# A two-layer hybrid encoder on one core: split matmuls reordered over PSUM banks, with a fourth pair of split weight buffers

## The chip, the cores and the metric

The kernel runs on one core of a Trainium2 chip. The metric is the device time of one execution in microseconds; lower is better. TensorE multiplies (the trace keeps its weight loads apart as PEld), VectorE (DVE), ScalarE (ACT) and GpSimd (POOL) do the rest, and SyncE (SP) issues the DMAs. PSUM has eight banks, named 0 to 7 in the code (`pb[b]`).

## What is computed

Two layers (`DEPTH = 2`), 512 tokens, width 1024, all in float32:

```python
n = rms_norm(h, norm_mix[l]);  p = n @ w_in[l]
h = h + concat(mla(p), gla(p), hgrn2(p)) @ w_mix_out[l]
h = h + memory_cross_attention(rms_norm(h), rms_norm(mem), ...)   # 4 heads, 256 memory tokens
gate, up = split(rms_norm(h) @ w_ffn_in[l])                       # 2 x 2816 columns
h = h + (silu(causal_conv3(gate) + b) * up) @ w_ffn_out[l]
```

The mixer has three parts: a latent attention with low-rank q and kv, and two gated linear recurrences.

## The kernel before, in words

**Products in three parts.** A float32 product is made from two numbers for each operand, hi (`fp32r`, what TensorE keeps of the value) and lo (the rest). `product` (line 594) issues three matmuls into one bank, one after the other: hi x hi (line 597), hi x lo (line 598), lo x hi (line 599). The trace names them by these lines. Each matmul has its own weight load.

**Weight slabs.** The weights come as a list of slabs (`slabs`, lines 89 to 175) of at most 1024 columns per partition, in the order of use. A slab goes through three steps, each on its own engine:

- SP loads it into one of RAW = 3 raw buffers (line 511) as soon as the slab three back has been split;
- ScalarE copies it to `w_hi` (line 938), when the slab SPLIT = 3 back is released, that is, when TensorE has issued its last matmul with it;
- GpSimd subtracts to get `w_lo` (line 552), and only then may TensorE use the slab (`use`, line 588).

ScalarE and GpSimd do this between their other work, in an order written out by hand. `ahead(name)` (line 941) in ScalarE's program splits up to slab `name + SPLIT - 1`, which waits for the release of the slab before `name`.

**Who multiplies.** Two helpers do nearly all of the split products:

- `feature_chunk` (line 619) makes 128 output features for all 512 tokens in one bank: 8 steps of k, 24 matmuls in a row into the same bank. It makes the latents, the features of the recurrences, and the FFN's gate and up chunks. In the FFN there are two groups g of 11 pairs; pair n writes the banks 4g + 2(n mod 2) for gate and the next one for up (lines 912 to 919), each finished and released by itself.
- `token_group` (line 630) makes up to 512 output columns for each of four token tiles t (two for the memory) in four banks. For each k it goes through the tiles, with three matmuls for each, so the bank changes every third matmul. It makes the q, kv, v, r (`br`) and c,i,g (`cig`) projections, the mix, cross-attention and FFN outputs.

`claim(b)` waits until bank b has been read by its last reader. In a token group it stands before a tile's first product. A tile's last product signals its reader: VectorE adds the bank to h (`add_to_h`, line 1284), or ScalarE copies it out.

**The q/k stage.** Behind the kv projections VectorE prepares q and k for eight token tiles in turn (lines 1317 to 1367), and ScalarE makes a small step for each (line 1058); before each of these steps stands one `ahead` (lines 1050 to 1058). Meanwhile TensorE makes the features, then the v, r and c,i,g groups. The r group uses banks 0 to 3, of which bank 1 is read by VectorE (line 1360) in this chain. After the c,i,g group ScalarE evicts it (lines 1088 to 1091) and TensorE turns q and k.

**The FFN round.** For a chunk n VectorE multiplies the gate bank by the norm (line 1493), makes the convolution (lines 1495 to 1498), reads the up bank (line 1501), multiplies (line 1503) and makes a_lo (line 1505). ScalarE's program for n is: `ahead(gate)`, `ahead(up)`, silu (line 1208), a_hi (line 1210).

Elsewhere: `transpose_h` (line 601) turns h after the additions for the next norm; `y_ready` (line 837) turns the recurrences' output before the second half of k in the mix projection.

Of the kernel before, what the change touches and what calls it, by code (L numbers as in the profile page):

```python
# [27 lines left out]
def build_trunk(nc, A, out):  # L28
# [11 lines left out]
    P = 128  # L40
# [3 lines left out]
    NT, KD, MT = SEQ // P, D // P, NM // P  # L44
# [12 lines left out]
    FCG = FC // FG  # L57
# [31 lines left out]
    slabs, slab_at = [], {}  # L89
# [83 lines left out]
        for half in range(2):  # L173
            half_of(("ffo", g), A["w_ffn_out"], FCG, half, k0=g * FCG)
    NS = len(slabs)
    RAW, SPLIT, SLAB = 3, 3, 1024

    with ExitStack() as ctx:

# [37 lines left out]
        x_hi = place("x_hi", 0, [P, KD, SEQ], f32r)  # L217
        x_lo = place("x_lo", 16, [P, KD, SEQ], f32r)
# [65 lines left out]
        pb = [ctx.enter_context(nc.psum_tensor(f"bank{i}", [P, 512], f32)) for i in range(8)]  # L284
# [12 lines left out]
        S = {n: ctx.enter_context(nc.semaphore(n)) for n in names}  # L297
# [190 lines left out]
        with nc.Block() as block:  # L488
# [82 lines left out]
            released = {}  # L571

            @block.tensor
            def _(pe):
                freed, count = {}, {}

                def mark(ins, sem):

                    ins.then_inc(sem, 1)
                    count[id(sem)] = count.get(id(sem), 0) + 1  # L580
                    return sem, count[id(sem)]

                def claim(b):

                    if b in freed:
                        pe.wait_ge(*freed[b])

                def use(name):
                    i = slab_at[name]
                    nk, cols, _ = slabs[i]  # L590
                    pe.wait_ge(S["lo_split"], i + 1)
                    return [w[i % SPLIT][:, 0:nk * cols].rearrange("p (k c) -> p k c", k=nk) for w in (w_hi, w_lo)]

                def product(o, a, b, first, last):

                    (ah, al), (bh, bl) = a, b
                    pe.matmul(o, ah, bh, start=first, stop=False)  # L597
                    pe.matmul(o, ah, bl, start=False, stop=False)  # L598
                    return pe.matmul(o, al, bh, start=False, stop=last)  # L599
# [19 lines left out]
                def feature_chunk(name, b, w, done, evac, cols=P):  # L619

                    claim(b)
                    wh, wl = use(name)
                    for k in range(KD):
                        pe.wait_ge(S["x_lo_done"], w * KD + k + 1)
                        mm = product(pb[b][0:cols, :], (wh[:, k, :], wl[:, k, :]), (x_hi[:, k, :], x_lo[:, k, :]),
                                     k == 0, k == KD - 1)
                    released[slab_at[name]] = mark(mm, done)
                    freed[b] = evac

                def token_group(names, b0, cols, x, k0, ready, done, evac, nt=NT, before={}):  # L630

                    xh, xl = x
                    nk_all = sum(slabs[slab_at[n]][0] for n in names)
                    k = 0
                    for i, n in enumerate(names):
                        if i in before:
                            before[i]()
                        wh, wl = use(n)
                        for kk in range(slabs[slab_at[n]][0]):
                            if ready is not None:  # L640
                                pe.wait_ge(*ready(k))
                            for t in range(nt):
                                if k == 0:
                                    claim(b0 + t)
                                mm = product(pb[b0 + t][:, 0:cols],
                                             (xh[:, k0 + k, t * P:(t + 1) * P], xl[:, k0 + k, t * P:(t + 1) * P]),
                                             (wh[:, kk, :], wl[:, kk, :]), k == 0, k == nk_all - 1)
                                if k == nk_all - 1:
                                    last = mark(mm, done)
                            k += 1  # L650
                        released[slab_at[n]] = last if k == nk_all else mark(mm, S["slab_used"])
                    for t in range(nt):
                        freed[b0 + t] = (evac[0], evac[1] + t + 1)
# [59 lines left out]
                for t in range(NT):  # L713
                    mm = pe.transpose(pb[6][:, t * ROPE:(t + 1) * ROPE], rope_lr[0:ROPE, t * P:(t + 1) * P], ident[0:ROPE, 0:ROPE])
# [197 lines left out]
                for g in range(FG):  # L912
                    for c in range(FCG):
                        n = g * FCG + c
                        b = 4 * g + 2 * (n % 2)
                        feature_chunk(("gate", g, c), b, 2, S["ffn_mm"], (S["gate_ready"], n + 1))
                        feature_chunk(("up", g, c), b + 1, 2, S["ffn_mm"], (S["act_ready"], n + 1))
                        if n == 0:
                            spread_r(1)
                    for half in range(2):  # L920
                        project(("ffo", g), FCG, lambda k: (S["a_lo_done"], g * FCG + k + 1), (a_hi, a_lo),
                                (2 + g) * H_ADDS, half)
# [620 lines left out]
```

## Time and profile before

| | |
|---|---|
| median of 3 runs | 1568.45 us (1568.07 to 1570.29) |
| profiled execution: span from first to last instruction | 1568.1 us |
| profiled execution: time around the span | not listed apart; its span equals the lowest run to 0.1 us |
| TensorE busy | 1477.2 us, 94% |
| VectorE, ScalarE, GpSimd busy | 783.0, 596.9 and 638.7 us |
| granted TensorE clock | 0.982 of 2.4 GHz on average |

The busy time of TensorE counts matmuls that overlap each other, each from its start to the modelled end of its last column; two starts of neighbours are nearer to each other than one matmul is long. The pace is therefore read from starts, and the standstills from the gaps. A row's bracket names the idle time before it and what ended it.

### The profile page before, as it was taken

How to read it: one execution, taken by the hardware profiler on the slowest of the kernel's cores; microseconds unless marked ns; L12 is line 12 of the kernel's file. 1: busy time of each engine (PE TensorE's matmuls, PEld its weight loads, DVE VectorE, ACT ScalarE, POOL GpSimd, SP SyncE). 2: the span in 40 equal slices, each digit the busy share in tenths (PEclk: the TensorE clock that was granted, in tenths of full speed). 3: DMA queues.
4: the chain of work that ended last, by engine and by line, in shares of the span. 5: the costliest groups of instructions: out<-in, count | busy, mean ns of one | idle time of the engine just before them, and what ended most of it. 6: DMA issues, size and time to landing. Idle time of an engine off the chain costs nothing. (4 is left out here: it accounts for less than half of the span.)

```text
span 1568.1 us, 18614 instructions
## 1 busy us (share of the span) xinstructions
PE 1477.2 (94%) x6967; PEld 1196.0 (76%) x6967; DVE 783.0 (50%) x1505; ACT 596.9 (38%) x1053; POOL 638.7 (41%) x338
## 2 busy tenths in 40 slices
PE   6997889999999999999989898889999999999997
PEld 5886657787788888888868775678867888888886
DVE  4289468335376504653133965772345663055620
ACT  5524554457433212232154146633564322122220
POOL 5433621453343444444335254423523444444342
PEclk9998999999999999999999899999999999999999
DMA  5322001332233233333143220012322332333321
GB/s 146 96 80 68 27 1 41 94 108 68 81 94 94 88 101 95 94 94 100 35 118 95 68 81 1 1 65 84 118 68 70 95 106 88 90 106 89 99 87 74
DMA packets 172975, 125.81 MB, mean 80 GB/s; under 512 B 11825, under 2 KB 149840, under 8 KB 172880
## 3 DMA queue, kind: packets, MB, share of 16 engines
q1 hardware_dynamic: 172880, 124.56, 26.7%
q8 instruction: 58, 0.95, 0.2%
q14 instruction: 37, 0.30, 0.1%
HBM read 122.44 MB, written 2.10 MB: 79 GB/s over the span
## 5 line engine op out<-in xcount | busy, mean ns | idle before, releaser
L552 POOL TENSOR_TENSOR w_lo<-raw,w_hi 128x1024 fp32r<-128x1024 f32 (+2 forms) x230 | 544.5, 2371 | 789.2 <-ACT w_hi L938 789.1
L938 ACT ACTIVATE w_hi<-raw 128x1024 fp32r<-128x1024 f32 (+2 forms) x230 | 236.7, 1033 | 354.6 <-PE bank L599 349.0
L597 PE MATMUL bank<-x_hi,w_hi 128*128 128x512 f32 (+1 forms) x880 | 349.7, 397 | 0.3 <-DVE x_lo L1221 0.3
L598 PE MATMUL bank<-x_lo,w_hi 128*128 128x512 f32 (+1 forms) x880 | 347.8, 395 | 0.0
L599 PE MATMUL bank<-x_hi,w_lo 128*128 128x512 f32 (+1 forms) x880 | 347.8, 395 | 0.0
L597 PEld LDWEIGHTS bank<-x_hi,w_hi 128*128 128x128 f32 (+1 forms) x880 | 164.7, 187 | 41.7 <-issue 1.0
L598 PEld LDWEIGHTS bank<-x_lo,w_hi 128*128 128x128 f32 (+1 forms) x880 | 164.7, 187 | 41.0 <-issue 1.0
L599 PEld LDWEIGHTS bank<-x_hi,w_lo 128*128 128x128 f32 (+1 forms) x880 | 164.7, 187 | 40.7
L597 PE MATMUL bank<-w_hi,x_hi 128*128 128x512 f32 (+1 forms) x448 | 168.7, 376 | 18.7 <-POOL w_lo L552 12.5
L1289 DVE TENSOR_TENSOR h<-h,bank 128x512 f32<-128x512 f32 x64 | 44.0, 688 | 250.3 <-PE bank L599 250.2
L599 PE MATMUL bank<-w_hi,x_lo 128*128 128x512 f32 (+1 forms) x448 | 165.2, 369 | 0.0
L598 PE MATMUL bank<-w_lo,x_hi 128*128 128x512 f32 (+1 forms) x448 | 165.2, 369 | 0.0
L599 PE MATMUL bank<-w_hi,a_lo 128*128 128x512 f32 x352 | 138.7, 394 | 0.0
L598 PE MATMUL bank<-w_lo,a_hi 128*128 128x512 f32 x352 | 138.0, 392 | 0.0
L597 PE MATMUL bank<-w_hi,a_hi 128*128 128x512 f32 x352 | 136.6, 388 | 0.0
L1497 DVE SCALAR_TENSOR_TENSOR conv<-gate_in,gains,conv 128x512 f32<-128x512 f32 x44 | 120.3, 2733 | 1.6
L597 PEld LDWEIGHTS bank<-w_hi,x_hi 128*128 128x128 f32 x448 | 88.1, 197 | 36.8 <-POOL w_lo L552 14.2
L599 PEld LDWEIGHTS bank<-w_hi,x_lo 128*128 128x128 f32 x448 | 87.7, 196 | 14.0
L598 PEld LDWEIGHTS bank<-w_lo,x_hi 128*128 128x128 f32 x448 | 88.2, 197 | 12.9
L1208 ACT ACTIVATE conv_silu<-conv 128x512 f32<-128x512 f32 x44 | 27.8, 632 | 178.4 <-DVE conv L1498 178.4
L1493 DVE TENSOR_TENSOR gate_in<-bank,r_bc 128x512 f32<-128x512 f32 x44 | 30.4, 692 | 112.0 <-PE bank L599 112.0
L598 PEld LDWEIGHTS bank<-w_lo,a_hi 128*128 128x128 f32 x352 | 66.1, 188 | 15.5
(266 smaller groups left out, 1930.6 us busy)
## 6 DMA issues: line engine op xcount, KB each, us to landing
raw<-in_w_ffn_in SPq DMA_DIRECT2D x88, 512.0 KB, 3.8
raw<-in_w_ffn_out SPq DMA_DIRECT2D x40, 512.0 KB, 3.7
raw<-in_w_in SPq DMA_DIRECT2D x36, 512.0 KB, 3.7
raw<-in_w_mix_out SPq DMA_DIRECT2D x16, 512.0 KB, 3.8
raw<-in_w_ca_kv SPq DMA_DIRECT2D x32, 256.0 KB, 3.3
raw<-in_w_ca_q SPq DMA_DIRECT2D x8, 512.0 KB, 3.9
raw<-in_w_ca_out SPq DMA_DIRECT2D x8, 512.0 KB, 3.8
h<-in_x SPq DMA_DIRECT2D x4, 512.0 KB, 5.0
```

Of the source, the lines that this page charges most:

```text
L552: pool.tensor_tensor(w_lo[i % SPLIT][:, 0:n], raw[i % RAW][:, 0:n], w_hi[i % SPLIT][:, 0:n].bitcast(f32), ALU.subtract).then_inc(S["lo_spl ...
L597: pe.matmul(o, ah, bh, start=first, stop=False)
L598: pe.matmul(o, ah, bl, start=False, stop=False)
L599: return pe.matmul(o, al, bh, start=False, stop=last)
L938: act_.activation(w_hi[k % SPLIT][:, 0:n], raw[k % RAW][:, 0:n], ACT.Copy).then_inc(S["hi_split"], 1)
L1208: act_.activation(conv_silu[n % 2][:, :], conv[n % 2][:, :], ACT.Silu).then_inc(S["silu_done"], 1)
L1289: dve.tensor_tensor(h[:, t, c], h[:, t, c], pb[PROJ_BANKS[base // H_ADDS][half] + t][:, :], ALU.add).then_inc(S["h_added"], 1)
L1493: dve.tensor_tensor(gi[:, CONV - 1:], pb[4 * g + 2 * (n % 2)][:, :], r_bc[:, :], ALU.mult).then_inc(S["gate_ready"], 1)
L1497: link(dve.scalar_tensor_tensor(cv[:, :], gi[:, t:t + SEQ], w_(t), cv[:, :], ALU.mult, ALU.add))
```

## The change

Four edits:

- `SPLIT` is 4 instead of 3: four buffers each of `w_hi` and `w_lo`, 8 KB more per partition. `ahead` and the releases follow from it. To make room, the kernel is built with `dynamic_dma_scratch_size=1024`.
- In `token_group` the loop over the three products stands outside the loop over the tiles: all four tiles get hi x hi, then all four hi x lo, then lo x hi, so each matmul writes another bank than the one before. All banks are claimed before the first product, and all tiles close in the last pass.
- A new `gate_and_up` makes both chunks of an FFN pair together: for each k and product first gate, then up, alternating between two banks. Both weights must be ready at its start, and both are released at its end.
- `feature_chunk` stays for the latents and the recurrences' features.

```diff
--- before.py
+++ after.py
@@ -173,7 +173,7 @@
         for half in range(2):
             half_of(("ffo", g), A["w_ffn_out"], FCG, half, k0=g * FCG)
     NS = len(slabs)
-    RAW, SPLIT, SLAB = 3, 3, 1024
+    RAW, SPLIT, SLAB = 3, 4, 1024
 
     with ExitStack() as ctx:
 
@@ -627,6 +627,24 @@
                     released[slab_at[name]] = mark(mm, done)
                     freed[b] = evac
 
+                def gate_and_up(g, c, b):
+
+                    n = g * FCG + c
+                    claim(b)
+                    claim(b + 1)
+                    gate_w, up_w = use(("gate", g, c)), use(("up", g, c))
+                    for k in range(KD):
+                        pe.wait_ge(S["x_lo_done"], 2 * KD + k + 1)
+                        for p, (side, x) in enumerate(((0, x_hi), (0, x_lo), (1, x_hi))):
+                            for w, bank in ((gate_w, b), (up_w, b + 1)):
+                                mm = pe.matmul(pb[bank][:, :], w[side][:, k, :], x[:, k, :], start=k == 0 and p == 0,
+                                               stop=k == KD - 1 and p == 2)
+                                if k == KD - 1 and p == 2:
+                                    name = ("gate", g, c) if bank == b else ("up", g, c)
+                                    released[slab_at[name]] = mark(mm, S["ffn_mm"])
+                    freed[b] = (S["gate_ready"], n + 1)
+                    freed[b + 1] = (S["act_ready"], n + 1)
+
                 def token_group(names, b0, cols, x, k0, ready, done, evac, nt=NT, before={}):
 
                     xh, xl = x
@@ -639,14 +657,16 @@
                         for kk in range(slabs[slab_at[n]][0]):
                             if ready is not None:
                                 pe.wait_ge(*ready(k))
-                            for t in range(nt):
-                                if k == 0:
+                            opens, closes = k == 0, k == nk_all - 1
+                            if opens:
+                                for t in range(nt):
                                     claim(b0 + t)
-                                mm = product(pb[b0 + t][:, 0:cols],
-                                             (xh[:, k0 + k, t * P:(t + 1) * P], xl[:, k0 + k, t * P:(t + 1) * P]),
-                                             (wh[:, kk, :], wl[:, kk, :]), k == 0, k == nk_all - 1)
-                                if k == nk_all - 1:
-                                    last = mark(mm, done)
+                            for p, (xs, ws) in enumerate(((xh, wh), (xh, wl), (xl, wh))):
+                                for t in range(nt):
+                                    mm = pe.matmul(pb[b0 + t][:, 0:cols], xs[:, k0 + k, t * P:(t + 1) * P], ws[:, kk, :],
+                                                   start=opens and p == 0, stop=closes and p == 2)
+                                    if closes and p == 2:
+                                        last = mark(mm, done)
                             k += 1
                         released[slab_at[n]] = last if k == nk_all else mark(mm, S["slab_used"])
                     for t in range(nt):
@@ -913,8 +933,7 @@
                     for c in range(FCG):
                         n = g * FCG + c
                         b = 4 * g + 2 * (n % 2)
-                        feature_chunk(("gate", g, c), b, 2, S["ffn_mm"], (S["gate_ready"], n + 1))
-                        feature_chunk(("up", g, c), b + 1, 2, S["ffn_mm"], (S["act_ready"], n + 1))
+                        gate_and_up(g, c, b)
                         if n == 0:
                             spread_r(1)
                     for half in range(2):
@@ -1530,7 +1549,7 @@
     from concourse import mybir
     from concourse.bass_utils import run_bass_kernel_spmd
 
-    nc = bacc.Bacc("TRN2", target_bir_lowering=False, num_devices=1)
+    nc = bacc.Bacc("TRN2", target_bir_lowering=False, num_devices=1, dynamic_dma_scratch_size=1024)
     arrays, aps = {}, {}
     for name in _INS:
         a = np.ascontiguousarray(inputs[name])
```

## Rows read from the trace of the kernel before

**Rows 1.** The page, part 1: busy time, share of the span, instructions

```profile
PE 1477.2 (94%) x6967; PEld 1196.0 (76%) x6967; DVE 783.0 (50%) x1505; ACT 596.9 (38%) x1053; POOL 638.7 (41%) x338
```

**Rows 2.** Timeline, FFN pair, VectorE, then GpSimd: start, length (us), engine, line

```profile
661.84 0.69 DVE L1493 TENSOR_TENSOR gate_in<-bank,r_bc 128x512 f32<-128x512 f32 x1 [2.79 <-PE bank L599]
...
663.15 2.83 DVE L1497 SCALAR_TENSOR_TENSOR conv<-gate_in,gains,conv 128x512 f32<-128x512 f32 x1
666.02 0.75 DVE L1498 SCALAR_TENSOR_TENSOR conv<-gate_in,gains,conv 128x512 f32<-128x512 f32 x1
667.44 0.69 DVE L1501 TENSOR_TENSOR up_s<-bank,r_bc 128x512 f32<-128x512 f32 x1 [0.67 <-PE bank L599]
...
673.04 0.69 DVE L1493 TENSOR_TENSOR gate_in<-bank,r_bc 128x512 f32<-128x512 f32 x1 [2.79 <-PE bank L599]
...
670.55 2.40 POOL L552 TENSOR_TENSOR w_lo<-raw,w_hi 128x1024 fp32r<-128x1024 f32 x1 [5.11 <-ACT w_hi L938]
```

**Rows 3.** Timeline, FFN output group of layer 1, TensorE

```profile
745.00 0.39 PE L599 MATMUL bank<-w_hi,a_lo 128*128 128x512 f32 x1
745.23 0.39 PE L597 MATMUL bank<-w_hi,a_hi 128*128 128x512 f32 x1
...
746.83 0.39 PE L598 MATMUL bank<-w_lo,a_hi 128*128 128x512 f32 x1
```

**Rows 4.** Timeline and groups by shape: fp32 product of probabilities and values

```profile
1155.29 1.88 PE L689 MATMUL bank<-cprobsT,ckv_tok 128*128 128x512 f32 x4
...
L689 PE MATMUL bank<-cprobsT,ckv_tok 128*128 128x512 f32 x32 | 14.7, 593 | 0.0
```

**Rows 5.** Groups by line and shape, TensorE: count, busy us, mean ns, idle before

```profile
L597 PE MATMUL bank<-x_hi,w_hi 128*128 128x512 f32 x864 | 343.3, 397 | 0.0
...
L597 PE MATMUL bank<-w_hi,a_hi 128*128 128x512 f32 x352 | 136.6, 388 | 0.0
L597 PE MATMUL bank<-w_hi,x_hi 128*128 128x512 f32 x320 | 129.7, 405 | 7.9 <-POOL w_lo L552 6.2 <-DVE x_lo L1280 1.4 <-DVE x_lo L1221 0.4
```

**Rows 6.** Timeline, end of an up chunk, start of the next gate chunk, TensorE

```profile
667.01 0.40 PE L599 MATMUL bank<-x_hi,w_lo 128*128 128x512 f32 x1
667.24 0.39 PE L597 MATMUL bank<-x_hi,w_hi 128*128 128x512 f32 x1
```

**Rows 7.** Timeline, mix projection in the first and the second layer, TensorE

```profile
287.03 0.39 PE L597 MATMUL bank<-w_hi,x_hi 128*128 128x512 f32 x1
...
289.32 0.39 PE L598 MATMUL bank<-w_lo,x_hi 128*128 128x512 f32 x1
...
1069.15 0.40 PE L597 MATMUL bank<-w_hi,x_hi 128*128 128x512 f32 x1
...
1071.02 0.40 PE L599 MATMUL bank<-w_hi,x_lo 128*128 128x512 f32 x1
```

**Rows 8.** Timeline, h additions at the end of the first layer, VectorE

```profile
781.82 2.75 DVE L1289 TENSOR_TENSOR h<-h,bank 128x512 f32<-128x512 f32 x4 [27.46 <-PE bank L599]
```

**Rows 9.** Timeline, transposes of h after the cross-attention output, TensorE

```profile
413.74 1.97 PE L608 MATMUL bank<-ident,h 128*128 128x128 f32 x16 [0.78 <-DVE h L1289]
```

**Rows 10.** Timeline, eviction of the v group, second layer, ScalarE

```profile
850.36 2.75 ACT L1044 ACTIVATE v_tok<-bank,small 128x512 f32<-128x512 f32 x4 [1.80 <-PE bank L599]
```

**Rows 11.** Timeline, r and c,i,g groups of the second layer, TensorE

```profile
897.81 0.58 PE L597 MATMUL bank<-w_hi,x_hi 128*128 128x256 f32 x1 [2.06 <-DVE K L1360]
...
920.53 0.50 PE L597 MATMUL bank<-w_hi,x_hi 128*128 128x512 f32 x1 [2.60 <-POOL w_lo L552]
...
938.72 0.60 PE L733 MATMUL bank<-ident,q_tok 128*128 128x128 f32 x4
```

**Rows 12.** Stretches: length, busy us (count) of the engines, granted clock, DMA

```profile
898.00:904.00 6.00, 6.00 (x29) 6.00 (x30) 5.33 (x20) 1.45 (x3) 2.38 (x1) 0.51 0.00 1
```

**Rows 13.** Timeline, before the second half of mix, TensorE, then VectorE

```profile
1052.91 3.07 PE L843 MATMUL bank<-ident,o_tok 128*128 128x128 f32 x16 [2.13 <-POOL w_lo L552]
...
1050.68 2.72 DVE L1443 TENSOR_TENSOR o_tok<-o_tok,sg_tok 128x512 f32<-128x512 f32 x1
```

## Prediction

> **What bounds the kernel now.** I read the busy shares first: TensorE is busy 94% of the span [rows 1], so I ask what sets its pace and where it stands still. The timeline of its matmuls gives the pace. In the gate/up chunks VectorE takes up a new gate chunk every 11.20 us (661.84, then 673.04) [rows 2], and 48 matmuls lie between, so one 128x512 matmul starts every 233.3 ns. In the FFN output groups eight steps take 1.83 us (745.00 to 746.83) [rows 3], 229 ns each. The streaming itself, 512 columns at 2.4 GHz, is 213.3 ns. The fp32 matmuls come close to their streaming time: four of them take 1.88 us, of which the last one's length is 0.59, so they step by 0.43 us [rows 4], twice 213.3 ns and 2.5 ns over. So 13 to 17.5 ns per matmul of the split (hi/lo) products is what this change could win, if the bank has to do with it. The counts by shape say how many there are, in triples of the three products: 864 in the feature chunks (704 of them the 88 gate and up chunks of 8 triples), 352 in the FFN output, 320 in the other 512-column token groups that read x [rows 5]; by the code the memory and latent groups add 96.
>
> **Part 1: the order in which banks are written.** The old order already contains bank changes, and the trace shows what they cost or save. Every 24 matmuls a chunk ends and the next one starts in another bank: that step is 667.01 to 667.24, 0.23 us [rows 6], the same as the step inside a chunk, and the 11.20 us of a pair, which contains two such changes, leaves no room for a shorter one. In a token group every third step changes the bank: 745.00 (third product) to 745.23 (first product of the next token tile) is 0.23 us as well, and the mean stays 229 ns [rows 3]. More: the same loop with the same bank changes ran at 229 ns in the first layer's mix projection (287.03 to 289.32, ten steps) and at 234 ns in the second layer's (1069.15 to 1071.02, eight steps) [rows 7]. So the excess is there with a bank change and without, and it differs where the bank order doesn't. And the fp32 matmuls of [rows 4], which accumulate in one and the same bank back to back, have almost none of it. I take **0 ns** as the gain per matmul from the new bank order, and keep both ends: the whole excess (rival 1) and the other level, 4 ns more or less (rivals 2 and 4). The number of weight loads doesn't change; each matmul has its own before and after.
>
> The Trainium skill ("TensorE: Matmul & The Clock Gate", Back-to-back issue gap) puts the gap between 512-column matmuls at 512/2.4 + 2.5, some 216 ns, and has no term for the bank. The fp32 rows agree with that form, the split products with 229 to 234 ns do not; if the new order brought them to it the result would be rival 1's.
>
> **Part 2: closing a token group.** In the old order tile t is finished three matmuls after tile t-1, so the first of four banks is ready 9 matmuls before the end; in the new order all four close in the last pass, one matmul apart, the first of them 3 before the end. The first eviction starts 6 x 0.229 = 1.37 us later relative to the group's end. Four h additions take 2.75 us [rows 8], 0.69 each, which is three matmuls: before, they kept step with the closing; now they queue behind each other and the last one ends 1.4 us later. That costs where TensorE waits for all four. Three places per layer: the cross-attention output before the transposes of h (TensorE waits 0.78 us there now [rows 9]), the last FFN output before the end of the layer [rows 8], and the second gate (c, i, g) group before ScalarE evicts and q is turned. The v group's eviction, too (850.36 us, ScalarE, four in 2.75 us, waiting for TensorE) [rows 10], feeds the long VectorE chain of q/k preparation, which starts behind it. Elsewhere another group of 11 us or more lies over the additions. The new order also claims four banks before the first product. That matters in one place, the r group, where today three matmuls go ahead and then wait until 897.81 us for a bank [rows 11]; the first three are lost, 0.7 us at most.
>
> **Part 3: a fourth split buffer.** ScalarE's split of slab i+3 (before: i+2) now goes ahead at the same place in its queue, since the release that it waits for is the same one. That helps where TensorE waits for a split held up behind something else in ScalarE's queue, the q/k preparation. The last such wait ends at 920.53 us, 2.60 us long, and the tokens' projections end at 938.72 [rows 11]. With one slab more in hand this wait and the one before the first c,i,g slab fall away and TensorE is bound by the bank claim at 897.81 + 1.4 = 899.2. From there: the first r slab has 48 matmuls of 256 columns, at first at the lower clock of 1.2 GHz that holds there now after the standstill (granted 0.51 from 898 to 904 [rows 12]). If it holds 6 us again, 27 matmuls run at 256/1.2 = 0.213 us and the other 21 at 0.117 (half the 512-column step and a little), and the slab ends near 907.5. The second takes 5.6 us (913), and four slabs of 24 x 0.229 = 5.5 us each end at 935.2. That is 3.5 us before 938.7. Less the 1.37 us of the later eviction it leaves -2.1 us, and for the first layer, where the waits are alike, the same.
> In the mix projection TensorE waits 2.13 us for a split (1052.91) [rows 13]. But VectorE's last step of o, which the same transposes need, ends at 1050.68 + 2.72 = 1053.4 [rows 13], because it ran into a GpSimd split; the two new splits will stand in the same place. So only the three first transposes move up: -0.3 us.
>
> **Part 4: gate and up as one pair.** Both weights are released only at the pair's end. Here is what has to fit into one pair of 11.2 us. ScalarE's order is: split of the gate chunk two ahead, silu, a_hi, and only then the split of the up chunk two ahead. Today the last split of this round ends at 670.55 + 2.40 = 672.95, 11.1 us after VectorE took up the gate (661.84) [rows 2]. Of these, 0.67 us were VectorE's wait for up (667.44) [rows 2], which goes, since up ends 0.2 us after gate. So the up split is ready 10.4 us after the gate product's end, 10.2 after the pair's end, and TensorE needs it 11.2 after. It fits with **1.0 us** to spare: 0 us. The later start of VectorE's work (by 5.6 us) is hidden by the next pair, and at the last chunk by 27 us of output products before its tile is read. DMA queue: each load waits for the split three slabs back, as before; the latest one has most of a pair to land. The smaller DMA scratch gives room for the buffers and no queue of this kernel's GpSimd issues loads: 0.
>
> **The sum** per layer: -2.1 (q/k stage, closing included) - 0.3 (mix) + 1.4 (cross-attention output) + 1.4 (layer end) = +0.4; two layers +0.8 us. Bounds from the parts alone: if the q/k gain is all there and the closings hidden, -8; if the gain isn't there and all closings count, +8. The sum is made against the profiled execution's span of 1568.1 us, which is the lowest of the three runs to 0.1; the median is 0.3 above it. I say 1569.
>
> **The rivals.**
> 1. *The bank does cost.* The excess goes: FFN chunks 2112 x 17.5 ns = 37 us, 512-column groups 2304 x 13 ns = 30 us, together -67: about 1502 us. For it: the excess is there, and no row shows a stretch in which every neighbour changes bank. Against it: [rows 3, 4, 6, 7]. The pair would then take 10.4 us, and the up split at 10.2 would still just fit. Chance 0.16.
> 2. *Another level.* TensorE's step has two levels, 229 and 233.3 ns, which the old order doesn't explain; the new order might put the gate/up pairs on the lower: 2112 x 4.2 ns = -9, 1560 us, or a part of the excess may go, down to 1546. Chance 0.13.
> 3. *The up split comes late* (ends slower). Its place is ScalarE's queue behind a_hi. VectorE's second convolution step takes 2.83 us when it meets a GpSimd split, its twin 0.75 [rows 2]; one more such meeting adds 2.1 us to a chain that has 1.0 to spare. It decides from 11.2 us on. Each microsecond beyond it is paid half per pair (the pair after next shifts, and two share it): 1.1/2 x 44 = +24, 1593 us. Against: the second GpSimd split of a round starts after VectorE's chain is through. Chance 0.08. The Trainium skill ("SBUF — State Buffer", Who interferes with whom) says that a VectorE operation with two SBUF inputs and a GpSimd one that reads SBUF block each other for the whole instruction; the 2.83 against 0.75 us agrees.
> 4. *The token groups land on the upper level*, as the second layer's mix did: 2304 x 4.2 ns = +9, 1578 us. Chance 0.10.
>
> **The numbers.** My forecast, the step unchanged and the sum near zero, has 0.53, with 1561 to 1576 as its own range. The 8 in 10 range takes in rivals 2 and 4 and leaves out rival 1 and most of 3: 1545 to 1580. About 0.2% (3 us) is what a measurement of this kernel can tell from no change. Faster: rivals 1 and 2 and a fifth of the forecast, 0.39. Slower: rivals 3 and 4 and some of the forecast, 0.29. Same: 0.32.
>
> **What would show it.** Right: the FFN chunks still give a gate every 11.2 us with the two banks alternating; the waits for splits in the q/k stage gone or short, its projections ending some 3 us earlier in the stage; transposes of h after the cross-attention output waiting 2.2 us in place of 0.8. Wrong: a pair of 10.4 us (rival 1), 11.0 (rival 2), or TensorE waiting on a w_lo split at each pair (rival 3).

## The result, and the profile after

The changed kernel takes **1588.51 us** (median of 4 runs, 1587.64 to 1590.23), the kernel before 1569.37 us in the same comparison (4 runs, 1568.07 to 1571.15): ratio 1.012, 95% interval 1.0106 to 1.0135. It is slower by 19 us. 1569 us was forecast, and the range ended at 1580. The profiled execution took 1590.23 us with a span of 1588.37, 20.2 above the span of before (1568.14).

The page of the changed kernel, busy time (answers to [rows 1]):

```profile
PE 1481.9 (93%) x6967; PEld 1200.1 (76%) x6967; DVE 769.3 (48%) x1505; ACT 595.7 (38%) x1053; POOL 636.1 (40%) x338
```

TensorE is busy 4.7 us longer and idle 15.5 us longer: its work has hardly grown, and most of the loss is standing still. The gate/up pairs, timeline of VectorE and GpSimd (answers to [rows 2]):

```profile
665.45 0.69 DVE L1512 TENSOR_TENSOR gate_in<-bank,r_bc 128x512 f32<-128x512 f32 x1 [3.42 <-PE bank L640]
...
676.65 0.69 DVE L1512 TENSOR_TENSOR gate_in<-bank,r_bc 128x512 f32<-128x512 f32 x1 [3.42 <-PE bank L640]
...
673.53 2.41 POOL L552 TENSOR_TENSOR w_lo<-raw,w_hi 128x1024 fp32r<-128x1024 f32 x1 [4.49 <-ACT w_hi L957]
```

The pair still takes 11.20 us, although neighbours now write different banks throughout. The up split is ready at 675.94, 10.5 us after the gate was taken up, 0.7 before the next gate.

So the time is lost elsewhere. I cut both traces at the starts of TensorE's stretches and took, for each, how much later (+) or earlier (-) it passes from one mark to the next than before, layer 1 then layer 2. The v group (`bv` in the code) is the one before the r group (`br`):

| stretch, from mark to mark | forecast per layer | layer 1 | layer 2 |
|---|---|---|---|
| layer start to the v group | 0 | +1.00 | +0.97 |
| v, r, c,i,g, q turned | -2.1 | -2.75 | -2.83 |
| to the second half of mix | -0.3 | +0.06 | +0.51 |
| second half of mix to the cross-attention query group | 0 | +4.06 | +2.68 |
| from there to the cross-attention output group | 0 | +4.12 | +4.08 |
| from there to the first gate chunk | +1.4 | +1.51 | +1.06 |
| FFN to the layer's end | +1.4 | +2.79 | +2.96 |

The sum is +20.2. The fourth and fifth lines, with 14.9 of it, were not in the forecast at all; nor was the first, with 2.0. TensorE's timeline shows what stands there in the first layer: the first memory half, the query group, the second memory half, the output group and the transposes after it (the last row answers to [rows 9]):

```profile
319.35 0.70 PE L666 MATMUL bank<-w_hi,m_hi 128*128 128x512 f32 x2 [1.00 <-DVE m_lo L1473]
...
334.65 1.49 PE L666 MATMUL bank<-w_hi,x_hi 128*128 128x512 f32 x4 [2.32 <-DVE x_lo L1240]
...
359.29 0.71 PE L666 MATMUL bank<-w_hi,m_hi 128*128 128x512 f32 x2 [0.82 <-ACT cq_tok L1188]
...
394.49 1.16 PE L666 MATMUL bank<-w_hi,x_hi 128*128 128x512 f32 x4 [1.72 <-DVE x_lo L1299]
...
420.36 3.46 PE L608 MATMUL bank<-ident,h 128*128 128x128 f32 x16 [1.88 <-DVE h L1308]
```

In the fourth line the first memory half begins 1.17 us later in each layer and the query group 2.57 later again; the rest, +0.4 in one layer and -1.0 in the other, lies in the first 120 products behind the mark, which take 28.4 and 27.9 us here and took 28.0 and 28.9 before. Before the change, the query group waited 0.18 us when six products had gone ahead, the output group 0.69 when three had, and the second memory half not at all:

```profile
332.27 0.48 PE L597 MATMUL bank<-w_hi,x_hi 128*128 128x512 f32 x1
...
334.09 0.50 PE L597 MATMUL bank<-w_hi,x_hi 128*128 128x512 f32 x1 [0.18 <-DVE x_lo L1221]
...
388.00 0.47 PE L597 MATMUL bank<-w_hi,x_hi 128*128 128x512 f32 x1
...
389.62 0.50 PE L597 MATMUL bank<-w_hi,x_hi 128*128 128x512 f32 x1 [0.69 <-DVE x_lo L1280]
```

What holds the query group is in the code. The transposes of h before it write the banks in the order 0, 1, 2, 3, 6, 7, 2, 3, so banks 2 and 3 are the last that VectorE's x_lo step frees. The old loop began on bank 0 and came to bank 2 six products later, 1.82 us after its start, just when it was freed; bank 3 comes one x_lo step later, 0.69 us. A group that claims all four first has to start 1.82 + 0.69 = 2.5 us later, and it starts 2.57 later.

The standstill has a second price. Stretches of 6 us from the start of the query group and from the start of the transposes after the output group; after the length stand the busy times of TensorE, its weight loads, VectorE, ScalarE and GpSimd, then the granted clock (the last two numbers are the DMA's). First the kernel before:

```profile
332.27:338.27 6.00, 5.82 (x27) 4.46 (x26) 2.42 (x4) 5.89 (x11) 0.00 (x0) 1.00 0.30 89
...
413.74:419.74 6.00, 6.00 (x34) 5.18 (x35) 2.73 (x4) 5.25 (x9) 0.00 (x0) 1.00 0.25 73
```

and the same two of the changed kernel:

```profile
334.65:340.65 6.00, 6.00 (x19) 4.79 (x20) 0.00 (x0) 5.87 (x11) 1.00 (x1) 0.72 0.13 38
...
420.36:426.36 6.00, 6.00 (x27) 5.48 (x28) 3.00 (x4) 4.53 (x7) 0.00 (x0) 0.72 0.08 23
```

The waits before them are 2.32 and 1.88 us, where they were under 0.8, and the clock is 0.72 in place of 1.00: a part of each stretch ran at 1.2 GHz. The query group gets 1.11 us longer (23.43 us from its first to its last start, 22.32 before), the sixteen transposes 1.5 (3.46 us, 1.97 before [rows 9]).

This price is not paid every time. In a repetition of the changed kernel (e9 below) the second layer's query group and transposes began after waits of the same length, and the clock stayed at 1.00:

```profile
1119.68 1.16 PE L666 MATMUL bank<-w_hi,x_hi 128*128 128x512 f32 x4 [2.32 <-DVE x_lo L1240]
...
1203.79 1.97 PE L608 MATMUL bank<-ident,h 128*128 128x128 f32 x16 [1.88 <-DVE h L1308]
```

```profile
1119.68:1125.68 6.00, 6.00 (x26) 4.96 (x27) 0.00 (x0) 5.87 (x12) 1.00 (x1) 1.00 0.14 41
1203.79:1209.79 6.00, 6.00 (x34) 5.18 (x35) 2.73 (x4) 5.24 (x9) 0.00 (x0) 1.00 0.07 21
```

That query group took 21.82 us, 0.5 less than before, where the short wait lay inside it. Against the 23.43 at the lower clock, the clock is worth 1.6 us there. Of the ten query groups in the five profiles with the claims up front (changed, e4, e5, e8, e9), seven took 23.4 us and three 21.8.

The fourth buffer does its work. TensorE's row at the r group, second layer (answers to [rows 11]):

```profile
910.77 1.20 PE L666 MATMUL bank<-w_hi,x_hi 128*128 128x256 f32 x4 [7.31 <-DVE K L1379]
```

The waits for splits are gone from the stage (before 6.3 us in three waits, after none), and they have run together into this one, which was 2.06. The c,i,g stretch behind it takes 21.99 us (924.31 to 946.30) where it took 26.56 (912.16 to [rows 11]'s 938.72): 4.57 less.

### The profile page after: what moved, and what is told of

Same layout as the page of the kernel before. It is cut to its first block, busy times and chain, and to the rows that moved or that the text cites. A ratio compares the mean times of both kernels' runs of the same rounds, so it can differ in the third digit from the quotient of the medians.

```text
span 1588.4 us, 18668 instructions
## 1 busy us (share of the span) xinstructions
PE 1481.9 (93%) x6967; PEld 1200.1 (76%) x6967; DVE 769.3 (48%) x1505; ACT 595.7 (38%) x1053; POOL 636.1 (40%) x338
## 4 chain that ended last, share of the span: by engine, by line
PE 38%; DVE 7%; ACT 3%; issue 1%; POOL 1%; DVEq 0%; ACTq 0%
PE bank L666 17%; PE bank L640 16%; PE bank L608 1%; PE bank L709 1%; PE bank L597 1%; PE bank L599 1%; DVE q_tok L1361 1%; PE bank L598 1%; DVE scores_h L1432 0%; DVE h L1308 0%; DVE scores_g L1432 0%; DVE junk_v L1351 0%; DVE small L1270 0%; PE bank L812 0%; DVE o_tok L1462 0%
## 5 line engine op out<-in xcount | busy, mean ns | idle before, releaser
L640 PE MATMUL bank<-x_hi,w_hi 128*128 128x512 f32 x704 | 223.0, 398 | 0.0
L640 PE MATMUL bank<-x_lo,w_hi 128*128 128x512 f32 x704 | 221.5, 396 | 0.0
L640 PE MATMUL bank<-x_hi,w_lo 128*128 128x512 f32 x704 | 221.4, 395 | 0.0
L640 PEld LDWEIGHTS bank<-x_hi,w_hi 128*128 128x128 f32 x704 | 132.5, 189 | 32.6 <-issue 1.0
L640 PEld LDWEIGHTS bank<-x_lo,w_hi 128*128 128x128 f32 x704 | 132.5, 188 | 32.3
L640 PEld LDWEIGHTS bank<-x_hi,w_lo 128*128 128x128 f32 x704 | 132.3, 188 | 32.0
L666 PE MATMUL bank<-w_hi,x_hi 128*128 128x512 f32 (+1 forms) x448 | 110.9, 371 | 22.7 <-DVE K L1379 14.6
L666 PE MATMUL bank<-w_lo,x_hi 128*128 128x512 f32 (+1 forms) x448 | 109.9, 369 | 0.0
L666 PE MATMUL bank<-w_hi,x_lo 128*128 128x512 f32 (+1 forms) x448 | 109.4, 367 | 0.0
L1227 ACT ACTIVATE conv_silu<-conv 128x512 f32<-128x512 f32 x44 | 27.9, 633 | 166.7 <-DVE conv L1517 166.7
L666 PEld LDWEIGHTS bank<-w_hi,a_hi 128*128 128x128 f32 x352 | 66.4, 189 | 15.1
```

What stands on the lines that cost most here:

```text
L640: mm = pe.matmul(pb[bank][:, :], w[side][:, k, :], x[:, k, :], start=k == 0 and p == 0, stop=k == KD - 1 and p == 2)
L666: mm = pe.matmul(pb[b0 + t][:, 0:cols], xs[:, k0 + k, t * P:(t + 1) * P], ws[:, kk, :], start=opens and p == 0, stop=closes and p == 2)
L1227: act_.activation(conv_silu[n % 2][:, :], conv[n % 2][:, :], ACT.Silu).then_inc(S["silu_done"], 1)
```

## The experiments

Two theories. **Edges:** the bank order is worth nothing, and all that is lost is lost where a token group opens (four claims before the first product) and closes (all four tiles in the last pass). **The rival:** inside the groups or pairs the new order itself costs, by its bank changes, or the fourth buffer or the pairs cost something that the whole hides. The kernel before is 1571.29 us in the first four comparisons (15 runs), 1570.9 in the next four (7), 1570.87 and 1570.28 in the last ones (7 each).

**e1_split4**, the kernel before with only the fourth buffer:

```
-    RAW, SPLIT, SLAB = 3, 3, 1024
+    RAW, SPLIT, SLAB = 3, 4, 1024
...
-    nc = bacc.Bacc("TRN2", target_bir_lowering=False, num_devices=1)
+    nc = bacc.Bacc("TRN2", target_bir_lowering=False, num_devices=1, dynamic_dma_scratch_size=1024)
```

> Only the fourth pair of split buffers (and the smaller DMA scratch), old matmul order everywhere. Theory E (edges: the loss comes from claiming all banks first and closing all banks last, the fourth buffer gains): 1557 to 1561 us, from the q/k stage, where the changed kernel's second c,i,g stretch was 4.5 us shorter in each layer, with none of the losses between mix and FFN. Rival S (the fourth buffer, through ScalarE's split order or the moved addresses, brings the loss): 1575 us or more.

Measured: 1560.46 us, ratio 0.9935 (0.9915 to 0.9955). The gain is real and worth 10.9 us in the stretch from the v group to q turned alone (-5.64 and -5.27). The waits before the slabs merge into one, for the bank that K frees (TensorE, second layer):

```profile
892.28 0.58 PE L597 MATMUL bank<-w_hi,x_hi 128*128 128x256 f32 x1 [5.77 <-DVE K L1360]
```

**e2_claims**, the changed kernel with each bank claimed before its own first product:

```
-                            if opens:
-                                for t in range(nt):
-                                    claim(b0 + t)
                             for p, (xs, ws) in enumerate(((xh, wh), (xh, wl), (xl, wh))):
                                 for t in range(nt):
+                                    if opens and p == 0:
+                                        claim(b0 + t)
```

> The changed kernel with each bank claimed just before its tile's first product, not all four ahead. The banks are then opened 1, 2 and 3 matmuls later, not 3, 6 and 9. Theory E: a small part comes back, 0.2 to 0.7 us at each of some five places per layer: 1582 to 1587 us. If the mere position of the claims is the cause and not the order of products: 1572 to 1577. Rival S: 1588.

Measured: 1580.21 us, ratio 1.0057 (1.0038 to 1.0077), 8.3 under the changed kernel: the claims up front cost, more than I gave them. The query group starts 2.56 us earlier relative to what comes before it (2.57 in the second layer), and the output group 1.93. The first rows of the query group:

```profile
329.09 0.71 PE L665 MATMUL bank<-w_hi,x_hi 128*128 128x512 f32 x2
330.91 0.50 PE L665 MATMUL bank<-w_hi,x_hi 128*128 128x512 f32 x1 [1.10 <-DVE x_lo L1239]
331.57 0.51 PE L665 MATMUL bank<-w_hi,x_hi 128*128 128x512 f32 x1 [0.16 <-DVE x_lo L1239]
```

Two products go ahead; but a pass over the tiles reaches the third bank after two products, not after six, so a wait of 1.10 is left.

**e3_close**, e2 with the last k written tile by tile, as before:

```
-                            for p, (xs, ws) in enumerate(((xh, wh), (xh, wl), (xl, wh))):
-                                for t in range(nt):
+                            order = [(p, t) for p in range(3) for t in range(nt)]
+                            if closes:
+                                order = [(p, t) for t in range(nt) for p in range(3)]
+                            for p, t in order:
+                                xs, ws = ((xh, wh), (xh, wl), (xl, wh))[p]
...
```

> As the run before, and the last k of every token group tile by tile, as in the old order, so that the banks close three matmuls apart. Theory E: the late closings come back, 1.4 us at the q/k turn, the layer end, before the FFN, and up to 2.1 at the memory keys and values: 1570 to 1576 us. A rival by which only the claims count: 1583 or more. Rival S: 1588.

Measured: 1565.46 us, ratio 0.996 (0.9948 to 0.9973): 14.7 under e2, lower than expected. The late closing had cost more than the claims, 13.2 us of span against 9.7. The q turn gives 1.37 us back in each layer, the six products of the forecast; the transposes of h after the output group come 1.1 earlier in both layers, the FFN's chunks from the second pair on another 1.6 in both, the first layer's end 1.56. The wait of the transposes is that of [rows 9] again, and so is their time:

```profile
411.52 1.97 PE L608 MATMUL bank<-ident,h 128*128 128x128 f32 x16 [0.78 <-DVE h L1310]
```

**e6_edges**, e3 with the first k tile by tile too, so that only the inner k of a group change the bank at each product; the pairs stay as changed:

```
-                            if closes:
+                            if opens or closes:
```

> As the run before, and the first k tile by tile too; only the k between keep the new order (alternating banks), and the gate/up pairs stay. Theory E: all edges are as in the old order; it should come within 2 us of the run with only the fourth buffer, 1558 to 1565 us. Rival B (the new order has a cost inside the groups): 1570 or more. Rival S: 1588.

Measured: 1558.98 us, ratio 0.9924 (0.9899 to 0.9948). That is the fourth buffer's time. All of the loss is at the edges.

**e8_tokens**, the other way round: the kernel before with three buffers, and of the change only the token groups' hunk:

```
+                            if opens:
+                                for t in range(nt):
+                                    claim(b0 + t)
+                            for p, (xs, ws) in enumerate(((xh, wh), (xh, wl), (xl, wh))):
+                                for t in range(nt):
...
```

> The kernel before with its three split buffers and only the token groups in the new order (three passes over four banks, all banks claimed first). The theory that the group's edges cost: the whole change is 28 us above the fourth buffer alone (1588.5 to 1560.5), and all of it is from here, so 1571.3 + 28 = 1599 us, a few us less where TensorE waits for a split at the same edge anyway: 1592 to 1600. If the loss comes from the fourth buffer and the order together, or from the pairs, this one lies below 1588 us.

Measured: 1593.9 us, ratio 1.0141 (1.0119 to 1.0164). **e7_pairs**, the kernel before with the fourth buffer and the pairs, without the new token groups:

```
-    RAW, SPLIT, SLAB = 3, 3, 1024
+    RAW, SPLIT, SLAB = 3, 4, 1024
...
-                        feature_chunk(("gate", g, c), b, 2, S["ffn_mm"], (S["gate_ready"], n + 1))
-                        feature_chunk(("up", g, c), b + 1, 2, S["ffn_mm"], (S["act_ready"], n + 1))
+                        gate_and_up(g, c, b)
```

> The kernel before with the fourth split buffer and the gate/up pairs, and with the old order in the token groups. By my theory the pairs cost nothing while they run (11.20 us a pair, the up split in time) and only the first one, which claims two banks and two weights at the start, can lose a little: 1560.5 (the fourth buffer alone) to 1563.5 us. If the pairs do cost where the comparison of the whole change didn't show it (rival), it lies above 1565 us.

Measured: 1561.28 us, ratio 0.9936 (0.9917 to 0.9955); 0.8 above e1. The pairs cost nothing. The stretches of the table above, both layers added, for the kernels that differ in the edges (profiled executions, against before):

| stretch | changed | e8 | e2 | e3 | e6 | e1 | e7 |
|---|---|---|---|---|---|---|---|
| layer start to the v group | +2.0 | +1.3 | +0.3 | +1.8 | +1.0 | -1.2 | -1.4 |
| v, r, c,i,g, q turned | -5.6 | +1.7 | -5.7 | -10.0 | -11.6 | -10.9 | -10.8 |
| to the second half of mix | +0.6 | +1.5 | 0.0 | +0.6 | 0.0 | +0.7 | +0.6 |
| to the query group | +6.7 | +6.9 | +1.6 | +1.6 | +0.5 | +0.6 | +1.2 |
| to the output group | +8.2 | +6.6 | +4.2 | +2.7 | 0.0 | +0.8 | +0.4 |
| to the first gate | +2.6 | +3.4 | +4.8 | +0.9 | +0.3 | 0.0 | 0.0 |
| FFN to the end | +5.8 | +2.3 | +5.4 | -0.1 | +0.1 | +1.3 | +1.2 |

Read along a line. The claims (changed to e2) are the 5.1 and 4.0 us before the query and the output group, of which 2.2 are given back before the gates. The closing (e2 to e3) is 4.3 by the q turn, 1.6 and 3.8 in the cross-attention, 5.4 in the FFN, where 1.2 are a level of the step (below). The opening pass (e3 to e6) is 1.6, 1.1 and 2.7; only the 2.7, by the output group, stands in both layers alike (1.35 and 1.34), while the 1.6 is all in the second layer and e1, with the same edges as e6, doesn't have it. The fourth buffer alone gives 10.9, and the edges eat half of that in the same stretch. In the first line 0.59 us of each layer is an effect of the claims: with all four banks claimed first the latent group's first product comes 0.74 to 0.77 us after the product before it (changed, e4, e5, e8, e9), else 0.15 (the other eight profiles). The changed kernel's row is

```profile
57.97 0.94 PE L666 MATMUL bank<-w_hi,lat_hi 128*128 128x384 f32 x4 [0.52 <-POOL w_lo L552]
```

The profile names a split as what ended this wait, but e2, which differs only in the place of the claims, has no such wait. Other differences up to some 1.6 in that line are no effect of the kernel: the latent group's first 48 products take 8.2 us from first to last start, with a clock of 1.00 over the first 6, or 9.8 with 0.72, in one layer or the other, in profiles of kernels that don't differ there.

**e4_pair_order**, the changed kernel with the bank changing at every third product of a pair:

```
-                            for w, bank in ((gate_w, b), (up_w, b + 1)):
+                        for w, bank in ((gate_w, b), (up_w, b + 1)):
+                            for p, (side, x) in enumerate(((0, x_hi), (0, x_lo), (1, x_hi))):
```

> The changed kernel, but each gate/up pair writes three products of one slice into one bank and then three into the other, so that the bank changes at every third matmul in place of every one (352 pairs of slices, 2112 matmuls a kernel). My theory (the bank of the neighbour costs nothing): the pair still takes 11.20 us (233.3 ns a step) and the time stays that of the changed kernel, 1586 to 1591 us. The rival (a bank change costs or saves something that the 233.3 ns hide on both sides) gives another step: with 4 ns a matmul either way, 11.0 or 11.4 us a pair and 1579 or 1597 us.

Measured: 1586.71 us, ratio 1.0092 (1.0064 to 1.0119), and VectorE takes up a gate every 11.20 us:

```profile
660.67 0.69 DVE L1512 TENSOR_TENSOR gate_in<-bank,r_bc 128x512 f32<-128x512 f32 x1 [3.43 <-PE bank L640]
671.87 0.69 DVE L1512 TENSOR_TENSOR gate_in<-bank,r_bc 128x512 f32<-128x512 f32 x1 [3.43 <-PE bank L640]
683.07 0.69 DVE L1512 TENSOR_TENSOR gate_in<-bank,r_bc 128x512 f32<-128x512 f32 x1 [3.42 <-PE bank L640]
```

**e5_one_bank**, the changed kernel with the FFN output groups' products all in one bank, so that the four token tiles' sums are added up in it and the FFN's part of h is another one:

```
...
-                                    mm = pe.matmul(pb[b0 + t][:, 0:cols], xs[:, k0 + k, t * P:(t + 1) * P], ws[:, kk, :],
-                                                   start=opens and p == 0, stop=closes and p == 2)
+                                    mm = pe.matmul(pb[b0 if one else b0 + t][:, 0:cols], xs[:, k0 + k, t * P:(t + 1) * P], ws[:, kk, :],
+                                                   start=opens and p == 0 and (not one or t == 0),
+                                                   stop=closes and p == 2 and (not one or t == nt - 1))
...
```

> The changed kernel with all products of an FFN output group written into one bank in place of four taking turns, so 352 of its 512-column matmuls never change the bank; the claims and the marks of the group are kept, the four token tiles' products are added up in that one bank, and so the FFN's contribution to h is another sum. If a neighbour in the same bank costs (the idea behind the change), the step of these groups goes from 229 ns (233 in one of the four) to more, and each 60.2 us group gets longer: the excess over 213.3 ns is 16 ns, and twice that would be +5.6 us for the kernel. My theory: the step stays at 229 or 233 ns, the four groups take 60.2 to 61.4 us each, and the time stays within 2 us of the changed kernel, except that the four tiles are all ready only at the last matmul (at most +0.5 us at each of the two layer ends). 1586 to 1592 us.

Measured: 1588.52 us, ratio 1.0115 (1.0098 to 1.0132). Four products in the same bank, 743.84 to 744.75, take 0.91 us, and four in four banks in the changed kernel, 751.01 to 751.92, 0.91 too (first fence e5, second the changed kernel):

```profile
743.84 1.07 PE L667 MATMUL bank<-w_hi,a_hi 128*128 128x512 f32 x4
744.75 1.08 PE L667 MATMUL bank<-w_lo,a_hi 128*128 128x512 f32 x4
```

```profile
751.01 1.07 PE L666 MATMUL bank<-w_hi,a_lo 128*128 128x512 f32 x4
751.92 1.08 PE L666 MATMUL bank<-w_hi,a_hi 128*128 128x512 f32 x4
```

**e9_after_again**, the changed kernel with no edit.

> The changed kernel once more, nothing edited. In the profiled execution of it the first layer's first FFN output group took 61.37 us (233 ns a step) and the second and third 60.22 (229). If the step's level belongs to the kernel's order or its addresses, the same groups take the same times again. My theory: the level belongs to the execution, so in this one another choice of the four groups and of the two mix groups is on 233 ns, and the span differs from 1588.4 us by the number of groups that changed times 1.16 us.

One execution: 1586.31 us, span 1584.5. (The groups of 60.2 or 61.4 us are both halves of an FFN output, 264 products.) The second layer's second one was at 233 ns in the profile of the changed kernel and is at 229 in this one; the first layer's first is at 233 in both. First fence the changed kernel, second the repetition, at about the same place of that group:

```profile
1541.26 1.10 PE L666 MATMUL bank<-w_hi,a_hi 128*128 128x512 f32 x4
1542.19 1.10 PE L666 MATMUL bank<-w_lo,a_hi 128*128 128x512 f32 x4
```

```profile
1538.03 1.07 PE L666 MATMUL bank<-w_hi,a_hi 128*128 128x512 f32 x4
1538.94 1.08 PE L666 MATMUL bank<-w_lo,a_hi 128*128 128x512 f32 x4
```

So the level is not fixed by the order or the addresses. But the span differs by 3.9 us and not by 1.16: the second layer's query group is 1.6 shorter as well, and what lies between its output group and the second gate/up pair 1.6. Both are the clock after the standstills, 0.72 in the one profile and 1.00 in the other. Profiles of one kernel differ by such amounts in place: line by line, both layers added, these two are up to 1.7 us apart, and a line of the second table is good to that.

**e10_split5**, e1 with a fifth split buffer:

```
-    RAW, SPLIT, SLAB = 3, 4, 1024
+    RAW, SPLIT, SLAB = 3, 5, 1024
```

> The kernel before with five split buffers (old order everywhere). With four of them no row of TensorE's waits names a split as the releaser, so a fifth has nothing to take away: 1558 to 1563 us, the same as with four (1560.5). If splits still held TensorE somewhere unseen, it would be under 1557 us.

Measured: **1582.6 us**, ratio 1.0078 (1.0056 to 1.0099). A miss by 20 us. The two places are the latent group and the q turn, where TensorE waits 3.80 and 7.25 us in the first layer, 3.90 and 6.03 in the second. ScalarE and GpSimd at the second one (TensorE's row first, then ScalarE, then GpSimd):

```profile
171.63 1.09 PE L733 MATMUL bank<-ident,q_tok 128*128 128x128 f32 x4 [7.25 <-ACT qT_n L1064]
...
156.87 2.02 ACT L938 ACTIVATE w_hi<-raw 128x1024 fp32r<-128x1024 f32 x2
...
167.03 1.06 ACT L938 ACTIVATE w_hi<-raw 128x1024 fp32r<-128x1024 f32 x1 [8.14 <-DMA raw<-in_w_mix_out]
...
157.09 3.52 POOL L566 TENSOR_TENSOR qk<-Q,K 128x1536 f32<-128x1536 f32 x1 [5.85 <-DVE Q L1377]
160.57 4.72 POOL L552 TENSOR_TENSOR w_lo<-raw,w_hi 128x1024 fp32r<-128x1024 f32 x2
```

With five buffers ScalarE's split of one slab more stands ahead of the evictions of c,i,g and of q. Its raw buffer comes free when GpSimd has split the slab three back, and GpSimd's product of Q and K stands before that split, at a fixed place in its queue. So the load is issued at 163.14, lands at 167.03, and the evictions wait behind the split. A buffer more on one side moves a wait for a load to the head of another engine's queue.

**e11_raw4**, e1 with a fourth raw buffer:

```
-    RAW, SPLIT, SLAB = 3, 4, 1024
+    RAW, SPLIT, SLAB = 4, 4, 1024
```

> The kernel before with four split buffers and four raw buffers in place of three. With five split and three raw buffers ScalarE stood at the head of its queue waiting for a load (8.7 us before 60.19, 8.1 us before 167.03), with the work that TensorE needs behind it. A raw buffer more lets a load start a split earlier. If loads still hold ScalarE back anywhere that TensorE feels with four split buffers, this one is faster than the fourth split buffer alone (1560.5): under 1557 us. My theory: nothing on TensorE's waits names such a place there, so 1558 to 1563 us.

Measured: 1559.74 us, ratio 0.9922 (0.9898 to 0.9946), as with the fourth split buffer alone. No version of mine beats that by more than can be measured: e1, e6, e7 and e11 lie within 2.3 us, and each beats both kernels. Five split and four raw buffers together were not tried.

## Why the prediction was wrong

**The step that failed** is in part 2, the costing of what a group's edges move, in two sentences.

The first is on the opening: the claims of four banks before the first product matter "in one place, the r group", where "the first three are lost, 0.7 us at most." The r group showed nothing of it (the 192 products of the v and r groups took 32.2 us from first to last start with the claims up front and 32.1 and 32.2 without, in e2). It mattered where TensorE comes to banks that x_lo or m_lo has just to free: 2.57 us before the query group and 1.93 before the output group in both layers, and, by the difference to e2, 0.8 before the first memory half and 0.6 before the latent group. The rows were there. The waits for x_lo, 0.4 and 1.4 us in all, stand in the last of [rows 5]; I took them for short waits and dropped them. But a wait of 0.18 us behind six products says that the bank came 1.8 us after the group began, and a loop that claims it first pays all of that.

The second is on the closing: "Elsewhere another group of 11 us or more lies over the additions." I asked which work covers an eviction and not who takes its bank. The second memory half takes banks 0 and 1 of the query group and waits 0.82 us for the second cq_tok. And neither sentence counted the clock: two standstills passed from under 0.8 to 2 us, and what came behind each ran on a clock of 0.72 in this execution, 1.1 and 1.5 us more. I had counted a lower clock in the r group, from [rows 12], and nowhere else.

Point by point:

- **Bank order, 0 ns a matmul** (part 1): right. Never changing within a group (e5), at every third and at every product of a pair (e4 and the changed kernel), and at every 24th (before): the step is 229 or 233 ns in all. Rivals 1 and 2 are out. The Trainium skill ("TensorE: Matmul & The Clock Gate", Back-to-back issue gap), with no term for the bank, is right in that, and its 216 ns came in none of these rows.
- **Late closing, 1.4 us in three places** (part 2): the size is right where only the wait moves (1.37 at the q turn, 1.36 and 1.10 at the two layer ends, 1.10 at the transposes of h). e3 puts all closings at 13.2 us of span, where the sum had 11.1: these three and the v eviction's 1.4 of part 3, twice. The rest came with the clock, the second memory half and an FFN group on the other level (1.2).
- **The fourth buffer** (part 3): right. The -3.5 us held the later v group's 1.4, so -4.9 for the buffer alone; e1 gives -5.6 and -5.3. The two closings in the stage, 1.4 + 1.4 by the forecast, are 2.3 and 2.0 from e2 to e3, 1.37 of them at the q turn. Net 2.8 gained where I had 2.1. The clock after the standstill was 0.60 over 6 us from 910.80, counted in from [rows 12].
- **Mix, -0.3**: the rows showed the right partner. The projection before ends 2.28 us earlier relative to the stage, TensorE then waits 2.34 for the last step of o, and the net is 0.1 and 0.5 us of loss.
- **Up split with 1.0 us to spare** (part 4): right, 0.7. Rival 3 did not come, and e7 shows no cost of the pairs.
- **Rival 4** is no case of this change: two of the four FFN outputs were at 233 ns, 2.3 us of the 20.2, and in e9, the same kernel, only one.
- **What would show it**: all three signs of being right came (a gate every 11.20 us; the projections 4.1 and 4.2 us earlier in the stage, counted from the v group; 1.88 us before the transposes, 2.2 forecast). The time was wrong all the same, since none of them looked at the cross-attention.

With the missed terms in (the fourth and fifth lines of the first table, 14.9 us), the sum would have been 1568.1 + 0.8 + 14.9 = 1584. Most of the 4.6 us that are left stand in the table's first line (2.0) and its last (3.0 above the forecast).

## What to carry to other kernels

When a loop over tiles is turned inside out, each tile's first and last instruction moves against its neighbours, and every claim and every release at the loop's edges has to be priced: go through the groups one by one and ask for each bank who frees it last and who takes it next, counting from the group's start and not from the wait that the trace shows. Where only the inside of the loop is to be reordered, keep its first and last step tile by tile: e6 is that, and it turned +1.2% into -0.8%. A deeper buffer helps until its work, hoisted in an in-order queue, waits for something that another queue's fixed order gives late.

## What the runs showed of the hardware

- Split products of 512 columns run at 229 ns or at 233 ns a step, for tens of microseconds on end, in the same place of the same kernel in one execution and another (60.2 or 61.4 us for 264 of them). The gate/up pairs were at 233.3 in every profile (112.0 us for 480 products in each layer's second FFN group). What decides it stays open.
- Waits of 2.3 and 1.9 us before the query group and before the transposes were followed by 6 us at a mean granted clock of 0.72 in both layers of the changed kernel's profile. In the second layer of its repetition the same two waits were followed by 1.00. Waits of 0.2 and 0.8 us in the same places were followed by 1.00 in the kernel before.
